# Attention by query block and two heads with a turned result, and the context rows of the second expert table summed on TensorE in four column groups

## The reference, cut to what matters

```python
def attend(q, k, v):                       # 16 query heads, 4 key heads, head width 64
    def block(qi):
        s = jnp.einsum('bqkgd,bskd->bkgqs', qi, k).astype(jnp.float32) * ATTN_SCALE
        p = jax.nn.softmax(s, axis=-1).astype(v.dtype)
        return jnp.einsum('bkgqs,bskd->bqkgd', p, v)
...
def peer_mixer(h, w_query, sub_keys, u_tab, v_tab):
    ...                                    # 8 heads x 16 best experts = 128 slots per token
    def block(args):
        xb, eb, gb = args
        a = jax.nn.gelu(jnp.einsum('td,thkd->thk', xb, u_tab[eb]), approximate=False)
        return jnp.einsum('thk,thkd->td', gb * a, v_tab[eb])
```

## Time and profile before

| what | value |
| --- | --- |
| runs, median of 3 (lowest to highest) | 5611.46 us (5600.64 to 5616.17) |
| profiled execution, span from first to last instruction | 5604.2 us |
| busy share PE, DVE, POOL, ACT | 81%, 66%, 39%, 25% |
| mean granted TensorE clock | 0.935 |
| HBM read | 1694.5 MB, 303 GB/s over the span |
| layer 0: heads, projections, attention (by first matmuls) | 455 to 820, 820 to 890, 890 to 1170 us |
| layer 1: attention | 3672 to about 3952 us |

### The profile page before, as it was taken

How to read it: one execution, slowest core, us unless ns; L and a number is a source line. 1 busy time by engine, 2 the same in 40 slices (tenths; PEclk the granted TensorE clock), 3 DMA queues, 4 the chain that set the end, 5 groups by cost and what they waited for, 6 DMA issues and landing times. The chain is left out here.

```text
span 5604.2 us, 60591 instructions
## 1 busy us (share of the span) xinstructions
PE 4557.5 (81%) x17704; PEld 2520.6 (45%) x17704; DVE 3712.8 (66%) x7028; ACT 1424.7 (25%) x3646; POOL 2184.8 (39%) x1826
## 2 busy tenths in 40 slices
PE   7889988888676777777787999888795878777776
PEld 6556655646343322222265566556463433223222
DVE  2357768867788766754532677788677877677545
ACT  2112213411011333333321112134100113333333
POOL 0002124642656454455400121246336554444554
PEclk9999998999888999999999999989897989999999
DMA  7755336785989999999967543457869889999998
GB/s 267 266 184 194 122 131 219 255 331 215 384 318 346 421 419 418 418 421 416 383 225 275 197 163 117 175 191 254 330 243 365 326 311 421 421 419 411 421 421 345
DMA packets 296082, 1703.74 MB, mean 304 GB/s; under 512 B 33360, under 2 KB 43216, under 8 KB 175696
## 3 DMA queue, kind: packets, MB, share of 16 engines
q0 software_dynamic: 258048, 1342.29, 61.3%
q1 hardware_dynamic: 23712, 338.18, 15.8%
q10 hardware_dynamic: 14000, 19.42, 1.0%
HBM read 1694.52 MB, written 5.24 MB: 303 GB/s over the span
## 5 line engine op out<-in xcount | busy, mean ns | idle before, releaser
L368 POOL DMA_INDIRECT arena<-in_peer_uv,eidx x1024 | 1184.3, 1157 | 1458.7 <-POOLq L367 1195.4
L2151 DVE SCALAR_TENSOR_TENSOR arena<-arena 128x1024 f32<-128x1024 f32 x384 | 470.6, 1225 | 349.9 <-DMA arena<-in_peer_uv,eidx 338.4
L861 PE MATMUL banks<-arena 128*128 128x512 f32 x896 | 502.1, 643 | 237.7 <-PEq L1473 234.2
L411 POOL DMA_INDIRECT arena<-in_peer_uv,eidx x384 | 490.3, 1277 | 501.0 <-POOLq L410 475.7
L863 PE MATMUL banks<-arena 128*128 128x512 f32 x896 | 477.8, 616 | 0.0
L834 PE MATMUL banks<-ring,arena 128*128 128x512 f32 x864 | 383.7, 599 | 110.0 <-PEq L816 110.0
L463 ACT ACTIVATE arena<-arena 128x1 f32<-128x1 f32 (+1 forms) x772 | 156.9, 203 | 1035.4 <-ACTq L462 1033.6
L861 PEld LDWEIGHTS banks<-arena 128*128 128x128 f32 x896 | 155.3, 198 | 549.7 <-issue 549.2
L468 ACT ACTIVATE arena<-ident,arena 128x128 f32<-128x128 f32 x832 | 333.6, 401 | 234.7 <-ACTq L467 230.2
L2151 DVE SCALAR_TENSOR_TENSOR ring<-ring,arena 128x1024 f32<-128x1024 f32 x192 | 235.4, 1226 | 211.1 <-DMA ring<-in_peer_uv,eidx 209.9
L2161 DVE SCALAR_TENSOR_TENSOR arena<-arena 128x1024 f32<-128x1024 f32 x256 | 306.9, 1225 | 95.3 <-DMA arena<-in_peer_uv,eidx 80.8
(11 more groups left out here) (303 smaller groups left out, 7763.1 us busy)
## 6 DMA issues: line engine op xcount, KB each, us to landing
ring<-in_wblk SPq DMA_DIRECT2D x160, 2048.0 KB
arena<-in_peer_uv,eidx POOLq DMA_INDIRECT x1408
arena<-in_lnrows ACTq DMA_DIRECT2D x6, 1024.0 KB, 9.5
arena<-in_sk ACTq DMA_DIRECT2D x4, 1024.0 KB, 7.4
hT<-in_peer_uv,eidx POOLq DMA_INDIRECT x192
ring<-in_peer_uv,eidx POOLq DMA_INDIRECT x192
x<-in_x_sample ACTq DMA_DIRECT2D x1, 2048.0 KB, 28.6
out<-arena ACTq DMA_DIRECT2D x4, 512.0 KB, 7.5
```

What stands on the lines that cost most here:

```text
L368: nc.gpsimd.indirect_dma_start(grow[j], None, ins["peer_uv"], bass.IndirectOffsetOnAxis(ap=eidx[:, n, r:r + 1].bitcast(U32), axis=0)).then ...
L411: nc.gpsimd.indirect_dma_start(gslot[j], None, ins["peer_uv"].rearrange("(e h) d -> e (h d)", h=2), bass.IndirectOffsetOnAxis(ap=eidx[:, n ...
L861: nc.tensor.matmul(banks[:, b, :], diag[n], row[:, 0:CB], start=start, stop=stop, skip_group_check=True).then_inc(diag_used, 1)
L2151: V.scalar_tensor_tensor(u, u, 1.0, h2[:, t - 2, :], ALU.mult, ALU.mult, accum_out=av[:, r:r + 1])
```

## The change

1. **Attention.** The loop is over 32 steps: a block of 128 queries and both heads of a pair. Scores of the two heads are issued one after the other on the two row halves of the array, first both 512-column parts, then both 128-column parts. Ten blocks are turned in three portions of 4, 4 and 2 through PSUM bank 4. The values are now stationary (64 columns, the two heads on the two column halves) and the turned probabilities moving, so the result comes out turned; the softmax sums are spread over partitions by a product with the identity; VectorE takes a 128 x 128 reciprocal and one product (`finish`) straight into `oattT`. GpSimd's copy, the turning of the result and its copies are gone. Queries are turned from `qkv` one block at a time, four steps ahead.
2. **Second table.** Rows are not weighted on VectorE. One fetch now brings, for 32 tokens, four slots each (`regroup` reorders row numbers and gates so, with 16 copies of 32 x 32; `ctx_ids` gives all 128 numbers at once, after the whole choice). `spread_weights` builds from the weights blocks of 32 stationary columns, and `ctx_group` multiplies four fetched rows with them, each into its own 32 columns of the array, in banks 6 and 7: 32 groups of 8 matmuls, from step 4 to step 30.
3. **First table.** The dot products need the token inputs in the same order: ScalarE's queue copies them by DMA (`replicate`) into two of the eight row buffers, so six are left for these rows. 7 rows in a head (two in its first level) for 6, 10 for 4 before the query norm, then 4 in each of steps 0 to 3. None are left for `one_mix(one_tile)`.

```diff
 GATE_ROWS = 24
-HEAD_ROWS = 6
+HEAD_ROWS = 7
 KEY_ROWS = 22
-QUERY_ROWS = 4
-UNIT_ROWS = 2
+QUERY_ROWS = 10
+STEP_ROWS = 4
+CTX_DOT_ROWS = 6
+REPS = 4
+QG = SLOTS // REPS
+BUILD = 4
...
+        gelu_step = (SLOTS - dots_end) // STEP_ROWS
+        assert dots_end <= SLOTS and (SLOTS - dots_end) % STEP_ROWS == 0 and 0 < gelu_step < STEPS // 2
+        def groups_by(n):
+            return max(0, QG * (n - gelu_step) // (STEPS - 1 - gelu_step))
...
+            def ctx_rows_in():
+                stage_rows(0, SLOTS)
+                for r in range(SLOTS):
+                    row_in(row_slot(0, r), 0, r)
+                for r in range(SLOTS):
+                    if r == CTX_DOT_ROWS:
+                        pool.wait_ge(reps_done, 1)
+                        pool.sem_inc(reps_done, -1)
+                    row_in(row_slot(1, r), 1, QG * (r % REPS) + r // REPS)
...
+                def score(n):
+                    p, qt = divmod(n, LT)
+                    b = p % 2
+                    lhs = [qTs[b][64 * half:64 * half + 64, qt * P:(qt + 1) * P] for half in range(2)]
+                    keys = [KT[64 * half:64 * half + 64, b, :] for half in range(2)]
+                    for half in range(2):
+                        nc.tensor.matmul(banks[:, 2 * half, :], lhs[half], keys[half][:, 0:LAT], start=True, stop=True)
+                    for half in range(2):
+                        nc.tensor.matmul(banks[:, 2 * half + 1, 0:P], lhs[half], keys[half][:, LAT:KEYS],
+                                         start=True, stop=True).then_inc(to_dve[2 * half], 1)
...
+                        for half in range(2):
+                            c = 1280 + (2 * b + half) * HD
+                            v = qkv[:, j, c:c + HD] if j < LT else vpast[:, c - 1280:c - 1280 + HD]
+                            nc.tensor.matmul(out_bank[half * HD:(half + 1) * HD, :], v, PT[n % 2][:, half * NT + j, :],
+                                             start=j == 0, stop=j == NT - 1)
+                    for half in range(2):
+                        last = nc.tensor.matmul(rec_bank[half * HD:(half + 1) * HD, :],
+                                                psum[n % 3][:, half:half + 1].to_broadcast([P, HD]), ident[:],
+                                                start=True, stop=True)
+                    last.then_inc(to_dve[1], 1)
...
+                    for half in range(2):
+                        for j in range(REPS):
+                            slot = row_slot(1, REPS * q + j)
+                            op = nc.tensor.matmul(banks[32 * j:32 * j + 32, 6 + half, :], weights[:, q % BUILD, j, :],
+                                                  grow[slot][:, half * CB:(half + 1) * CB],
+                                                  start=q == 0, stop=q == QG - 1, skip_group_check=True)
+                            if half:
+                                op.then_inc(row_free[slot], 1)
...
+                for n in range(STEPS):
+                    for half in range(2):
+                        pe.wait_ge(prob_ready[half], 1)
+                        pe.sem_inc(prob_ready[half], -1)
+                    turn(n, 0, 4)
+                    if n + 1 < STEPS:
+                        score(n + 1)
+                    turn(n, 4, 8)
+                    if n:
+                        weigh(n - 1)
+                    if n + LT in (4 * LT, 6 * LT):
+                        pe.wait_ge(qn_ready, 1)
+                        pe.sem_inc(qn_ready, -1)
+                    turn(n, 8, 10)
+                    for q in range(groups_by(n), groups_by(n + 1) if n + 1 < STEPS else QG):
+                        ctx_group(q)
+                weigh(STEPS - 1)
...
+                def regroup(dst, src):
+                    for j in range(REPS):
+                        for part in range(4):
+                            V.tensor_copy(dst[32 * part:32 * part + 32, QG * j:QG * (j + 1)],
+                                          src[32 * j:32 * j + 32, :].rearrange("p (q a) -> p q a", a=4)[:, :, part])
+                    dve.drain()
...
+                    for r in range(jobs["at"], jobs["at"] + count):
+                        slot, j = row_slot(0, r), r // QG
+                        if r % QG == 0:
+                            dve.wait_ge(rep_full[j % 2], 64)
+                            dve.sem_inc(rep_full[j % 2], -64)
+                        dve.wait_ge(row_full[slot], landed[l, 0, r])
+                        V.scalar_tensor_tensor(grow[slot], grow[slot], 1.0, rep[j % 2], ALU.mult, ALU.mult,
+                                               accum_out=av[:, r:r + 1]).then_inc(row_free[slot], 1)
+                        if r % QG == QG - 1 and j < 2:
...
+                            dve.drain().then_inc(reps_done, 1)
                     jobs["at"] += count
+                def weigh_rows():
+                    dve.wait_ge(gelu_ready, 1)
+                    dve.sem_inc(gelu_ready, -1)
+                    V.tensor_tensor(wv, av, gates[1], ALU.mult)
+                    dve.drain()
+                def spread_weights(k):
+                    dve.wait_ge(blocks_free, 1)
+                    dve.sem_inc(blocks_free, -1)
+                    V.tensor_tensor(blocks[k % 2].rearrange("p (q j t) -> p q j t", q=BUILD, j=REPS),
+                                    stripes.unsqueeze(1).unsqueeze(1).to_broadcast([P, BUILD, REPS, 32]),
+                                    wv.rearrange("p (j q) -> p q j", j=REPS)[:, BUILD * k:BUILD * (k + 1), :].unsqueeze(3)
+                                    .to_broadcast([P, BUILD, REPS, 32]), ALU.mult).then_inc(blocks_ready, 1)
...
                 softmax(gates[0])
+                regroup(gates[1], gates[0])
                 decays(0, 0)
...
+                def finish(n):
+                    p, qt = divmod(n, LT)
+                    arrived(1)
+                    V.reciprocal(sums_tile, rec_bank)
+                    dve.drain()
+                    V.tensor_tensor(oattT[:, p, qt * P:(qt + 1) * P], out_bank, sums_tile, ALU.mult
+                                    ).then_inc(out_free, 1)
+                built = 0
+                lowest(0)
+                for n in range(STEPS):
+                    if n + 1 < STEPS:
+                        lowest(n + 1)
+                    if n:
+                        finish(n - 1)
+                    if n < 14:
+                        head_norm(512 + 256 * (n // 7), 4, P, n % 7, *narrow)
+                        if n % 7 == 6:
+                            dve.drain().then_inc(qn_ready, 1)
+                    if n < gelu_step:
+                        ctx_rows(STEP_ROWS)
+                    elif n == gelu_step:
+                        weigh_rows()
+                    while built < QG // BUILD and n >= gelu_step and BUILD * (built - 1) <= groups_by(n):
+                        spread_weights(built)
+                        built += 1
+                finish(STEPS - 1)
                 phase_barrier(dve, "dve")
                 one_mix(one_tile)
```

More of the change, by code:

```diff
@@ L146, in build @@
         gsum = small[:, 232:240]
-        sums = [acc, arena[:, 28416:28416 + D]]
+        rep = [arena[:, 14336 + b * D:14336 + (b + 1) * D] for b in range(2)]
+        blocks = [acc[:, b * CB:(b + 1) * CB] for b in range(2)]
         modrows = arena[:, 0:4 * P]
@@ L379, in _ @@
[L379 to L393 removed]
+                        stage_rows(r, r + SLOTS // 2)
@@ new lines, in turn @@
+                def turn(n, first, last):
+                    claim(4)
+                    for c in range(first, last):
+                        half, j = divmod(c, NT)
+                        op = nc.tensor.transpose(at(4, c - first), pr[n % 2][half][:, j * P:(j + 1) * P], ident[:])
+                    if last == 2 * NT and n + LT < STEPS:
+                        p, qt = divmod(n + LT, LT)
+                        op = nc.tensor.transpose(query_bank, qkv[:, qt, p * P:(p + 1) * P], ident[:])
+                    op.then_inc(to_act[4], 1)
@@ L1391, in _ @@
+                weigh(STEPS - 1)
+                for half in range(2):
+                    pe.drain().then_inc(to_act[6 + half], 1)
+                for b in (0, 1, 2, 3, 5):
                     pe.sem_inc(bank_free[b], 1)
```

375 lines of the change are left out of this document (150 added, 225 removed).

## The result

The changed kernel takes **5689.56 us** (median of 4, 5681.51 to 5702.45) beside 5608.38 for the kernel before: ratio 1.015, interval 1.0134 to 1.0166. It is 81 us slower; 18 us faster was forecast, with a range up to 5665. Span of the profiled execution: 5689.5 us (5604.2 before).

A forecast was written before the change was run, and what follows sets the result against it. It took VectorE and TensorE both to be near the bound in the attention, with waits for each other. Terms 5 + 8 + 9.5 - 23 - 8.5 gave -9 us a layer, -18 for both: 5593 us, range 5550 to 5665.

The forecast's parts named there:

- (d): Attention: TensorE bounds most steps after VectorE's rows leave; 256 us against 279.7, -23 a layer (-35 to +5).
- the row supply: Attention steps: four fetches a group take 5 to 5.6 us of each 7.05, so GpSimd keeps up.
- signs of being wrong: Attention: groups of 3 us or more, two scores in 1.9 us, row waits at L1382, or long TensorE waits for probabilities.
- the 202 behind it: Attention's other 27 steps: 190 us at 7.05 each, plus 12 for waits and the end.
- six changes of shape: Each TensorE attention step: switches between work shapes at 0.19 us each, 1.2 us with rounding.
- the price of a whole tail: Attention: if mode changes drain TensorE for 0.27 us, steps are 0.5 us dearer, (d)'s saving about 13 us smaller.
- (a): Ahead of the heads: fetches start some 30 us later, rows end a little later; +5 us a layer (3 to 8).
- (b): Heads: a seventh row in each of 8 heads costs 1.0 of its 1.15 us; +8 us a layer.
- (c): Projection stage: six more rows 6.9, slower fetches with fewer buffers 3.5, copy gone -0.9; +9.5 a layer (5 to 12).
- (e): After the attention: `one_mix(one_tile)` has no rows left, weight waits shrink; -8.5 us a layer (-10 to -4).
- fetches bound the steps: Attention: GpSimd at 1.99 + 0.30 us a row needs 9.2 us a group, 294 us for 32; 5703, chance 0.04.
- rivals on TensorE: Attention: a dearer TensorE step, 5661 or 5673, chance 0.17; column groups working two at a time, 5703, chance 0.05.

The follow-up runs named there:

- constant_products: Changed kernel with 30 of 32 groups' matmuls run on columns of the keys, ahead of the waits for rows, table rows unused: 5625.17 us.
- half_rows: Changed kernel fetching only 64 of 128 second-table rows, each four fetched rows serving two groups, TensorE's work unchanged: 5609.51 us.
- late_groups: plain_dots with one group a step in steps 4 to 30 and the last five behind weight blocks of `one_mix(one_tile)`: 5562.94 us.
- plain_dots: Changed kernel with part 3 undone: first-table rows in the old order, eight buffers, no replicas, the 128 dot products reordered afterwards: 5646.07 us.
- six_rows: late_groups with gelu later, groups from step 6, six groups behind the attention, six rows a head and six in each of four steps: 5556.19 us.
- half_bytes_16: Changed kernel with second-table fetches of 2 KB instead of 4 KB per token, sixteen buffers, one wait per group: 5585.30 us.

## Why the prediction was wrong

- **(d), the row supply, is the step that failed.** It reads "4 fetches a group at 1.24 to 1.4 us are 5 to 5.6 for each 7.05, so GpSimd keeps up". The pace of issue was right (0.94 + 0.30 for nearly every fetch in the steps). What I left out is that with eight buffers for groups of four only two groups are under way, and a buffer is back in use only after the group has read it, four issues (5 us) and the landing, some 6 us. Waits for rows at L1382 stood among the signs of being wrong, but no term had a price for them. A warning was to be had from rows: the earlier trace rows showed the DMA engines 0.74 busy at 243 GB/s, so 328 GB/s if wholly busy (an estimate), and by that a fetch of 512 KB takes 1.6 us and four take 6.4, with nothing over for two groups in a step. It warns of the right place by the smaller cause, though: half the bytes gave back 7 and 13 us of the attention, twice the buffers beside that 42 and 38, and `constant_products` moves 343 GB/s from 1000 to 1150 us. I spread 32 groups over 27 steps as an average (32/27), where the real order makes five of them double, and a double step is just what a full loop can't take. Priced by `half_rows`: 35 to 37 us a layer, nearly the whole of the miss in the attention (-23 forecast, +15 and +16 measured). Some 10 of them are the lower clock behind the waits: by the sum used above TensorE loses 23 us to it in the changed kernel's attention and 13 in that of `half_rows`.
- The rest of (d) held in its terms, and its sum in part by luck: without row waits the attention takes 259 us for 256 forecast, made up of 40.5 for the 44 put ahead of step 4, 21.8 for the 10 put for step 4, and 197 for the 202 behind it. A reciprocal of 128 columns took 0.96 us (0.95 forecast), a group 1.85 to 1.92 (1.8), column and row halves work at once. The six changes of shape cost no more than the 0.19 each that I had put: the whole step runs in 6.2 to 6.3 us in `late_groups` where the terms gave 6.5 with one group, which leaves about 0.15 for a change (an estimate by the same terms). The Trainium skill, "TensorEngine Tiling (Array Packing)", Key Properties, says that a change of mode drains the engine; by the price of a whole tail that I gave it a step would take over 7 us, and the trace does not agree with that price. Step 4, with gelu, weights and first group, had no row behind its 10 us; in the changed kernel the gap between the scores is 22.0.
- **(a) failed by size:** +23 and +12 for +5 (13 to 23 and 10 to 19 over the six kernels with this order). I let 24 rows run at "1.25 to 1.3 us each"; VectorE waited for rows six times, 19.1 us in all, with the DMA engines 99% busy. In the old order that competition was there too, but the rows had 38 us more of a start. The old order (`plain_dots`) gives back 16 and 6.
- (b) +8 forecast, +8 and +12.5 measured; `six_rows` gives the same 10 from the other side. (c) +9.5 forecast, +14: six rows as priced, the two missing buffers and the copies 7.5 (`plain_dots`) in place of 3.5. (e) -8.5 forecast, -10 and -9.
- The rival "fetches bound the steps" named the right resource with the wrong cause (a slow issue, 1.99 + 0.30, where the fetches shown above took 0.94 to 1.08), so it got a chance of 0.04 and a time, 5703, that lies near the measured 5690 by accident. Its 55 us a layer don't follow from its 294 either: beside the 202 put for the 27 steps and their waits, 294 is 92 longer. The rivals on TensorE, with 0.22 together, played no part.

## What to carry to other kernels

Price a stream of buffers by its round trip (hold, issue of all that are given back together, landing), and by its rate in the stretch where it runs, not by the pace at which its issues can follow one another; then look for the places where the consumer asks for two at once, since an average over steps hides them. When work has been moved off the bound engine, ask what now stands at its limit, and fit the new work to that: here one group a step, with the surplus put behind weight blocks, and the old order of the first table, turned +81 us into -44 (0.9934 of the time before). Undo the convenient parts of a change one at a time: the reordered first table cost 43 us and was not needed.

## What the runs showed of the hardware

- Less work made the kernel slower, and more made it faster, where TensorE waits for something else: without its products it was granted 0.79 of its clock and the kernel took 5722 us; with as many products of constant data 0.96 and 5625. The lower clock itself is 22 of the 48 us between the two attentions of layer 0; the rest no run separates.
- Of the TensorE shapes: a group of 16 records of 512 columns over four column groups takes 1.85 us, four records of 512 over the two row halves 0.96, and a reciprocal of 128 x 128 on VectorE 0.96 (all `late_groups`).
- What stays open: in most steps of the changed kernel ScalarE's last copies start 1.7 to 2.5 us after the turning that they wait for, about when the group behind is done; in `late_groups`, `half_bytes_16` and `constant_products` they start after 0.49 us in nearly every step, in `half_rows` in about half of them. VectorE's reciprocal shows the same: 2.1 to 3.0 us behind the start of the last sum (L1365) in most steps of the changed kernel, 0.43 in `late_groups`. The instructions are the same. After:

```profile
1060.13 0.20 ACT L726 ACTIVATION_READ_ACCUMULATOR arena<-banks,small 128x1 f32 x1
1061.68 0.27 ACT L751 COPY arena<-banks 128x128 f32<-128x128 f32 x1 [1.34 <-ACTq L451]
```

  and in `late_groups`:

```profile
1044.14 0.21 ACT L733 ACTIVATION_READ_ACCUMULATOR arena<-banks,small 128x1 f32 x1
1044.23 0.27 ACT L758 COPY arena<-banks 128x128 f32<-128x128 f32 x1
```

  A single step takes 6.8 us with the late start and 6.2 with the early one, which would account for most of the difference between the 83 us that `late_groups` gained and the 56 expected. What decides between the two I can't say; no run was made for it.
